# Moving a triangular substitution from between the state transitions into the chunk chain of an RWKV-7 layer, with the sample's chunk last

## What is computed

```python
def step(state, inp):
    r_t, w_t, k_t, v_t, a_t, b_t = inp
    sa = jnp.einsum('bhvk,bhk->bhv', state, a_t)
    state = (state * w_t[:, :, None, :] + sa[..., None] * b_t[:, :, None, :]
             + v_t[..., None] * k_t[:, :, None, :])
    return state, jnp.einsum('bhvk,bhk->bhv', state, r_t)
```

## Time and profile before

| | us |
|---|---|
| median of 3 runs | 1527.07 (1525.47 to 1527.36) |
| the profiled execution | 1526.22 |
| its span, first to last instruction | 1524.5 |
| PE busy in the span | 1292.3 |
| DVE busy in the span | 886.5 |
| ACT busy in the span | 504.6 |
| the block of the change | about 868 to 995 of the span |

### The profile page before, as it was taken

One profiled execution on the slowest core, in us unless ns is written; L12 is line 12 of the kernel. 1 busy time (PEld: TensorE's weight loads), 2 busy tenths in 40 slices (PEclk: granted clock), 3 DMA queues, 4 the chain that ended last, 5 costly groups with the idle time before them and its releaser, 6 DMA issues. The chain is left out here.

```text
span 1524.5 us, 24643 instructions
## 1 busy us (share of the span) xinstructions
PE 1292.3 (85%) x10862; PEld 1224.4 (80%) x10862; DVE 886.5 (58%) x991; ACT 504.6 (33%) x524; POOL 50.0 (3%) x38
## 2 busy tenths in 40 slices
PE   4799999988079999993999526779999995999998
PEld 2799999964069999993897426759999994999998
DVE  4766534666936665346746697656665347666433
ACT  2433323304135333221354112234333322433232
POOL 0100000100001000000000400001000000100000
PEclk9899999976579999996998757779999997999998
DMA  5244444510014444442332000024544541454430
GB/s 178 87 155 163 165 164 154 188 56 10 0 56 138 158 162 166 163 153 83 118 119 76 5 9 3 5 69 139 166 165 166 166 138 33 150 164 162 162 136 32
DMA packets 98625, 174.63 MB, mean 115 GB/s; under 512 B 11412, under 2 KB 18732, under 8 KB 98534
## 3 DMA queue, kind: packets, MB, share of 16 engines
q1 hardware_dynamic: 98212, 173.19, 34.3%
q10 hardware_dynamic: 322, 0.10, 0.0%
HBM read 170.95 MB, written 2.33 MB: 114 GB/s over the span
## 5 line engine op out<-in xcount | busy, mean ns | idle before, releaser
L295 DVE TENSOR_TENSOR w_lo<-raw,w_hi 128x2048 fp32r<-128x2048 f32 (+1 forms) x104 | 237.8, 2287 | 319.8 <-ACT w_hi L281 319.6
L310 PE MATMUL PS<-mlp_x_hi,w_hi 128*128 128x288 f32 x1024 | 306.3, 299 | 12.4 <-DVE mlp_x_lo L383 6.8
L281 ACT ACTIVATE w_hi<-raw 128x2048 fp32r<-128x2048 f32 (+1 forms) x104 | 197.6, 1901 | 337.0 <-PE PS L312 336.1
L311 PE MATMUL PS<-mlp_x_hi,w_lo 128*128 128x288 f32 x1024 | 303.4, 296 | 0.0
L310 PE MATMUL PS<-ff_hi,w_hi 128*128 128x288 f32 x1024 | 303.1, 296 | 0.0
L312 PE MATMUL PS<-mlp_x_lo,w_hi 128*128 128x288 f32 x1024 | 302.3, 295 | 0.0
L311 PE MATMUL PS<-ff_hi,w_lo 128*128 128x288 f32 x1024 | 302.1, 295 | 0.0
L312 PE MATMUL PS<-ff_lo,w_hi 128*128 128x288 f32 x1024 | 301.1, 294 | 0.0
L310 PEld LDWEIGHTS PS<-mlp_x_hi,w_hi 128*128 128x128 f32 x1024 | 193.2, 189 | 15.3 <-issue 11.4
L312 PEld LDWEIGHTS PS<-mlp_x_lo,w_hi 128*128 128x128 f32 x1024 | 194.1, 190 | 0.0
L311 PEld LDWEIGHTS PS<-mlp_x_hi,w_lo 128*128 128x128 f32 x1024 | 193.6, 189 | 0.2
(11 more groups left out here) (369 smaller groups left out, 1452.0 us busy)
## 6 DMA issues: line engine op xcount, KB each, us to landing
raw<-in_w_up SPq DMA_DIRECT2D x64, 1024.0 KB, 5.3
raw<-in_w_down SPq DMA_DIRECT2D x64, 1024.0 KB, 5.1
raw<-in_attn_w_in SPq DMA_DIRECT2D x6, 1024.0 KB, 5.5
raw<-in_attn_w_out SPq DMA_DIRECT2D x4, 1024.0 KB, 5.1
raw<-in_rwkv_w_r SPq DMA_DIRECT2D x4, 1024.0 KB, 4.9
raw<-in_rwkv_w_k SPq DMA_DIRECT2D x4, 1024.0 KB, 5.2
raw<-in_rwkv_w_v SPq DMA_DIRECT2D x4, 1024.0 KB, 5.1
raw<-in_rwkv_w_o SPq DMA_DIRECT2D x4, 1024.0 KB, 5.0
```

The source lines that it names most:

```text
L281: nc.scalar.activation(w_hi[:, n % SPLITS, :, 0:width], raw[:, n % RAWS, :, 0:width], ACT.Copy) \
L295: nc.vector.tensor_tensor(w_lo[:, n % SPLITS, :, 0:width], raw[:, n % RAWS, :, 0:width], w_hi[:, n % SPLITS, :, 0:width].bitcast(F32), ALU ...
L310: nc.tensor.matmul(out, hi, rhs_hi(k), start=first and k == 0, stop=False)
L311: nc.tensor.matmul(out, lo, rhs_hi(k), start=False, stop=False)
```

## The change

The rows 13 to 30 of the sample's substitution leave the four transitions and go, in five pieces, behind `advance(1)` to `advance(5)`. The diagonal, the transposition and the copies of the sample's inverse come after `advance(7)`, and everything of the sample that needs the inverse follows there, on PE, DVE and ACT. The steps 1 to 7 of the prompt come first on PE, with `outputs(6)` and `outputs(7)` held back until the sample's products are copied out, since they use the same PSUM bank. The two `make_lo` of DVE go to the end of the block. ACT's program is the same as before.

```diff
@@ PE @@
                 mm.then_inc(rows_pe.sem, 1)
+                pe.wait_ge(rows_out.sem, rows_out.at(1))
+                for n in range(1, 6):
+                    step(n, 5)
+                    outputs(n)
+                step(6, 5)
+                step(7, 5)
                 pe.wait_ge(inverted.sem, inverted.at(2))
                 apply_sample(x_diag_s, bk_s[:, 0, :, :], 7, applied)
-                pe.wait_ge(rows_out.sem, rows_out.at(1))
-                step(1, 5)
-                outputs(1)
                 pe.wait_ge(spread_ak.sem, spread_ak.at(2))
                 pe.wait_ge(solved_out.sem, solved_out.at(5))
                 apply_sample(ak_diag_s, solved_s, 7, applied_k)
-                step(2, 5)
-                outputs(2)
                 pe.wait_ge(k_solved.sem, k_solved.at(5))
                 sample_products(...)
-                step(3, 5)
-                outputs(3)
                 pe.wait_ge(carried.sem, carried.at(5))
                 sample_products(...)
                 sample_products(...)
-                for n in range(4, 8):
-                    step(n, 5)
-                    if n == 6:
-                        pe.wait_ge(adds_out.sem, adds_out.at(5))
-                        pe.wait_ge(y_own_out.sem, y_own_out.at(5))
-                    outputs(n)
+                pe.wait_ge(adds_out.sem, adds_out.at(5))
+                pe.wait_ge(y_own_out.sem, y_own_out.at(5))
+                outputs(6)
+                outputs(7)
                 pe.wait_ge(stepped.sem, stepped.at(14))
                 step(8, 5)
@@ DVE @@
-                    substitute(inv_s, *((13, 17), (17, 21), (21, 26), (26, 31))[i])
-                diagonal(inv_s)
...
-                advance(1, 5, states[2], add[:, 1, :, :])
-                finish(0)
-                advance(2, 5, states[3], add[:, 2, :, :])
+                pieces = ((13, 16), (16, 19), (19, 22), (22, 26), (26, 31))
+                for n in range(1, 8):
+                    advance(n, 5, states[n + 1], add[:, n, :, :])
+                    if n <= len(pieces):
+                        substitute(inv_s, *pieces[n - 1])
+                    if n in (1, 3, 5):
+                        finish(n // 2)
+                diagonal(inv_s)
+                step(V.transpose(inv_back[:, :, :].rearrange("p s n -> p n s"), inv_s[:, :, :]))
+                for g in range(4):
+                    ins = V.tensor_copy(x_diag_s[group(g), :, group(g)], inv_back[group(g), 0:SSLOTS, :])
+                ins.then_inc(inverted.sem, 1)
...
                 dve.wait_ge(applied_k.sem, applied_k.at(5))
...
-                advance(3, 5, states[4], add[:, 3, :, :])
-                finish(1)
-                for n in range(4, 8):
-                    advance(n, 5, states[n + 1], add[:, n, :, :])
-                    if n % 2:
-                        finish(n // 2)
-                    if n >= 6:
-                        make_lo(dve, w_out + n - 6, early=True)
                 dve.wait_ge(adds_out.sem, adds_out.at(5))
                 dve.wait_ge(y_own_out.sem, y_own_out.at(5))
+                finish(3)
                 advance(8, 5, states["s1"], add_s)
                 finish(4)
+                for n in range(w_out, w_out + 2):
+                    make_lo(dve, n, early=True)
```

More of the change, by code:

```diff
@@ L2223, in _ @@
                 dve.wait_ge(y_own_out.sem, y_own_out.at(4))
-                advance(1, 5, states[2], add[:, 1, :, :])
-                finish(0)
-                advance(2, 5, states[3], add[:, 2, :, :])
+                pieces = ((13, 16), (16, 19), (19, 22), (22, 26), (26, 31))
[10 more added lines that the diff above has]
+                ins.then_inc(inverted.sem, 1)
+                step(V.tensor_tensor(carry_s[:, :, 0:N], pair_eye[:, :].unsqueeze(1).to_broadcast([P, C, N]),
+                                     last_decay[:, :, 8:9].to_broadcast([P, C, N]), ALU.mult))
                 dve.wait_ge(applied_k.sem, applied_k.at(5))
```

## The result

The changed kernel takes **1537.93 us** (median of 6 runs, 1536.07 to 1540.11); the kernel before, beside it, 1526.27. The ratio is 1.0073, 95% interval 1.0055 to 1.0090: slower by 11.7 us, where +8.6 was forecast, and inside the range. The profiled execution took 1540.11 us, with a span of 1538.3 us, against 1524.5 before.

What follows compares the result with a forecast made beforehand. It took DVE and the hand-offs between engines to set the block's pace, not PE's work. Step 1 -12.5, chain and sample +19.9, tail +1.2 made +8.6 us, so 1535.7 us against the median; range 1528.5 to 1540.5.

Steps and rivals of the forecast that it cites:

- main mechanism: 13.66 us of DVE work moves from the transitions, where PE waits for DVE, to the chain, where DVE waits for PE.
- Start of step 1: End of the transitions: step 1 of the chain starts at 953.1 instead of 965.60, 12.5 us earlier.
- it is the bound: Transitions: without the substitution, the cycle of PE's `adds` and ACT's copies sets the pace, 4.4 us each time.
- the rival with the chance of 0.04: Transitions stay as slow because something else holds them: step 1 at 959.65 instead of 953.1, 1542.2 us; chance 0.04.
- the half-way price: Transitions: step 1 at 953.1, the middle between 954.3 and about 951.9, the latter if PE is granted 2.4 GHz.
- Chain: Step 1 to the end of `advance(7)`: DVE is the bound at either clock level; 23.9 us, ending at 977.0.
- Sample: From `advance(7)` to step 8, with nothing covering the sample's chain: 16.6 us, step 8 at 993.6, 7.4 us later.
- The half-way price for the outputs: Sample's part: its two outputs priced half-way between 3.56 us at clock 0.50 and 1.8 at 1.00, the rest at 0.50.
- Tail: From step 8 to ACT's last copy: +1.2 us, half-way between the clock levels, with both `make_lo` hidden.
- the rival with half clock throughout: Whole block at clock 0.50: chain 23.9, sample 17.5, tail +2.8, step 8 at 995.7; +12.3 us, 1539.4 us; chance 0.23.
- the links: Chain, a sign: DVE's sums of the links 1 to 5 some 3.8 us apart with almost no idle time.
- the 3 us of idle time ahead of the sample: A sign: PE idle for 3 us ahead of the sample's first product, with the clock at 0.50 there.

Runs made afterwards that it cites:

- e2: The changed kernel with the five pieces (rows 13 to 30 of the sample's substitution) left out altogether; 1532.22 us, ratio 1.0036 to the kernel before.
- e1: The changed kernel with the five pieces put back between the transitions, the sample still last; 1534.47 us, ratio 1.0047 to the kernel before.
- e3: The changed kernel with products of the identity with ones put into PE's waits of the chain and the sample's part; 1533.72 us, ratio 1.0045 to the kernel before.
- e4: The kernel before with each of the sample's groups of products one step later on PE, step 1 ahead of the first; 1523.94 us, ratio 0.9985.
- e5: The kernel before with rows 8 to 12 of the sample's substitution moved ahead of the four sums of line 2175; 1521.12 us, ratio 0.9968.
- e8: The changed kernel without nearly all products of line 1943, three full-size identity products standing in per `adds`; 1541.92 us in one execution.
- e9: The changed kernel without nearly all products of line 1943, one full-size identity product standing in per `adds`; 1531.25 us in one execution.

## Why the prediction was right

**Direction and main mechanism** hold. The pieces do not fit (e2: 8.2 of 13.66 us show, where 10 had to vanish for a gain), nothing covers the sample behind the prompt (e1), and the half clock makes it dear (e3).

**Start of step 1: wrong.** Forecast -12.5, measured -8.05. The step that failed is "it is the bound", said of the cycle of `adds` and ACT's copies at 4.4 us: a link took 5.63 on average, with 3.9 us of gaps in the transitions. I had seen them only as uneven `adds`, a microsecond of margin. Before, the waits for DVE covered them, and when these went the gaps were late next. By e1, taking the pieces out of the transitions gave 2.13 us, where 6.6 were forecast; the rest of the 8.05, 5.92 us as in e4, is the first product's place in PE's queue, forecast at 5.9. So in the transitions the rival with the chance of 0.04 was nearer to the truth. Of the 4.45 us missed, 1.2 are the half-way price: the clock stayed at 0.50 from the second transition to step 1.

**Chain: nearly right.** 23.07 us from step 1 (957.10) to the end of `advance(7)` (979.75 + 0.42), forecast 23.9. The clock was at 1.00 for somewhat less than half of it, not 0.50 throughout as I chose, but DVE is the bound at either level, as the text said, so that hardly matters; the links average 3.7 us, forecast 3.85.

**Sample: right mechanism, one price too low.** 17.53 us from there to step 8 (997.70), forecast 16.6, and 17.5 with all prices at 0.50. The half-way price for the outputs was the error: the clock did not come back.

**Tail: mis-sized for the same reason.** +2.66, forecast +1.2, and +2.8 at 0.50. `make_lo` and `make_hi` were hidden as stated.

So the sum was not as good as its distance from the result. Forecast were -12.5 + 19.9 + 1.2 = +8.6, and the terms read from the profiled execution make -8.05 + 20.00 + 2.66 = +14.6: chain and sample miss by 0.8 and 0.9 us in opposite directions, but step 1 and tail by 4.45 and 1.46 in the same one. That execution was the slowest of six; by the medians the loss is 11.7, and that the forecast lies only 3.1 us below it is in part luck. Sample and tail went the way of the rival with half clock throughout, and its 1539.4 us lies nearer to the median (1.5 us) than the forecast's 1535.7 (2.2). Of the signs that were named, the links, the 3 us of idle time ahead of the sample and the hidden `make_lo` came; step 1 near 953 and step 8 near 993 did not (957.10 and 997.70).

## What to carry to other kernels

Work moved into "gaps" is free only where the engine's idle time in one link, at the pace that the link would have without it, is longer than the piece; e5 found such a gap and got its full worth. Before a filler is taken out, ask what it covered: here the old waits for DVE hid most of the gaps in PE's stream of small products, and the prompt's steps hid the sample's chain of hand-offs. A serial chain between engines belongs between the steps of another chain, and behind it it costs its full length, at the clock that its own waits leave.

## What the hardware showed that was not expected

- From gap to gap 128 small products came to PE in 3.67 to 3.85 us in the changed kernel, with gaps of up to 1.4 us that the profile calls "issue"; fewer products removed them (e8, e9). It is not one fixed rate: in e9 PE had 134 products from one group of carries to the next (938.71 to 941.77) in 3.06 us at 1.00, with no idle time called issue. That the gaps come from the fetching of instructions is the likely reading, as a packet of instructions moves ahead of the end of each, but no run changed the fetching itself.
- The clock was at 0.50 for 4.3 us of nearly unbroken work in the changed kernel (957.0 to 961.3) before it rose, and for 12 us in e4 (957 to 969). What decides it stays open.
